# Gate and up products of two feed-forward layers as seven block products in place of eight

## The chip, the cores and the metric

The kernel runs on one core of one Trainium2 chip. The metric is the device time of one launch in microseconds, as the median of several runs. TensorE does the matmuls, VectorE (DVE in the profile), ScalarE (ACT) and GpSimd (POOL) the elementwise work, and SyncE (SP) issues most of the transfers.

## What is computed

One step of a decoder layer (model width 1024) for 1024 prompt positions and 64 sample positions, 1088 tokens together. The two feed-forward half steps stand at its beginning and at its end:

```python
def ffn_half_step(x, g, wg, wu, wd):
    h = rmsnorm(x, g)
    return x + 0.5 * ((jax.nn.silu(h @ wg) * (h @ wu)) @ wd)

# D_MODEL = 1024, D_FF = 2816
yp = ffn_half_step(yp, ffn1_norm[l], ffn1_gate[l], ffn1_up[l], ffn1_down[l])
...  # input projection, windowed attention, conformer convolution, output projection, cross attention
yp = ffn_half_step(yp, ffn2_norm[l], ffn2_gate[l], ffn2_up[l], ffn2_down[l])
```

The same two steps run on the sample tokens. All data are float32.

## The kernel before

Activations lie transposed: a channel is a partition, `T` = 1088 tokens are the columns. The channels make `KT` = 8 row tiles of 128. The tokens are cut into `CHUNKS` of 384, 384 and 320 columns. A float32 product is made of three fast matmuls: each operand is split into a high part (rounded to the format of the fast matmul) and the rest. The normed activations are `hh` and `hl`, the weights `wh` and `wl`, the hidden values `hidh` and `hidl`. The helper `three` (lines 778 to 781) issues high x high (L779), low weight x high (L780) and high weight x low (L781).

A feed-forward layer (`ffn`, one function on each engine) runs over `FG` = 11 groups of 256 hidden channels, the first ten of ffn2 and all of ffn1 as a hardware loop. In a group TensorE does, for two halves `f` of 128 hidden channels and for each chunk, the gate product and the up product (8 row tiles x 3 matmuls each) into two PSUM banks, and then the down products: for 3 chunks x 8 output tiles, 2 x 3 matmuls into one of the four banks 4 to 7. Beside it ScalarE applies silu to the gate (L1420), VectorE multiplies it with up into `ht` (L1933), ScalarE casts `ht` to `hidh` (L1426), VectorE subtracts to get `hidl` (L1921), and adds half of each down product to `x` (L1945), which frees the bank.

Weights: SyncE loads units of 128 x 1024 elements (512 KB) into the two buffers `raw` (`ffn_loads`, L470). GpSimd makes the high part with a cast (L718) and the rest with a subtraction (L720); `wh` and `wl` have four slots for gate and up, `bh` and `bl` two for down. All order comes from semaphores; each engine runs its own program. Before ffn1 TensorE transposes the convolution cache (`turn_cache`, L979) between the memory projections and the transposes of their results (L962); VectorE copies it to `Us`. After ffn1 comes a barrier and a norm, whose squares ScalarE makes (L1399) and TensorE sums (L788).

## Time and profile before

| | |
|---|---|
| median of 3 runs | 2730.72 us (2728.26 to 2732.05) |
| span of the profiled execution | 2729.7 us |
| TensorE busy | 2606.0 us, 95% |
| VectorE busy | 1085.0 us, 40% |
| GpSimd busy | 696.3 us, 26% |
| ScalarE busy | 546.1 us, 20% |
| ffn1 and ffn2, first matmul to last | about 99 to 891 us and 1902 to 2711 us |

The profile is of one execution. A line of a list of groups gives line, engine, operation, the output and input tiles, how often, then busy time and mean duration of one, then the idle time before them and what ended it. A line of a timeline gives start and duration in us. Matmuls overlap each other, so the sum of their durations is more than the time that they take. Spans on GpSimd are rough.

### The profile page before, as it was taken

Reading aid. Unit: us, or ns where it says so; the run is one execution under the profiler, and the core shown is the slowest. Engines: PE = TensorE matmul, PEld = TensorE weight load, DVE = VectorE, ACT = ScalarE, POOL = GpSimd, SP = SyncE. Lnnn points to the kernel's source line nnn. Section 1 sums busy time; section 2 is a strip of 40 time slices with the busy share of each in tenths; the row PEclk is TensorE's granted clock in tenths of the full one; section 3 lists DMA queues with packets and bytes.
Section 4 is the critical chain, followed back from the end, with each engine's and each line's share of the span. In section 5 each row is a group of like instructions: output and inputs, shape, how many; then the busy total and the mean of one; then the engine's idle time right before and its main releaser. Section 6 shows DMA issues by size and latency. Waiting matters only on the chain.

```text
span 2729.7 us, 42372 instructions
## 1 busy us (share of the span) xinstructions
PE 2606.0 (95%) x16775; PEld 2450.1 (90%) x16775; DVE 1085.0 (40%) x2019; ACT 546.1 (20%) x1307; POOL 696.3 (26%) x404
## 2 busy tenths in 40 slices
PE   7899999999999899979999999899899999999998
PEld 6899999999999799957557999679899999999998
DVE  5233323233332699544434343544422223233324
ACT  4200000000000415256323122321200000000002
POOL 6633222333223133123001220112333222333320
PEclk9999999999999999979999999999999999999999
DMA  6411111111111012145674223731111111111101
GB/s 214 130 46 42 38 43 46 46 46 38 38 46 46 16 46 94 43 170 171 258 287 134 62 72 122 291 127 46 47 46 42 38 42 46 46 46 46 38 23 66
DMA packets 208235, 224.48 MB, mean 82 GB/s; under 512 B 9978, under 2 KB 181558, under 8 KB 204051
## 3 DMA queue, kind: packets, MB, share of 16 engines
q1 hardware_dynamic: 191655, 195.45, 21.9%
q10 hardware_dynamic: 16492, 27.82, 2.7%
q8 instruction: 60, 0.98, 0.1%
q14 instruction: 28, 0.23, 0.0%
HBM read 190.84 MB, written 32.40 MB: 82 GB/s over the span
## 4 chain that ended last, share of the span: by engine, by line
PE 87%; DVE 6%; issue 3%; ACT 2%; DMA 2%; DVEq 0%; POOL 0%; SPq 0%; ACTq 0%; POOLq 0%
PE ps L779 25%; PE ps L781 24%; PE ps L780 24%; PE ps L1171 1%; PE ps L1215 1%; PE ps L1185 1%; PE ps L1099 1%; DVE hidl L1921 1%; PE ps L1112 1%; PE ps L1281 1%; PE ps L1264 1%; DVE ps L2017 1%; PE ps L1082 1%; DMA cK<-in_cache_mem_k 1%; DVE x L1945 0%
## 5 line engine op out<-in xcount | busy, mean ns | idle before, releaser
L779 PE MATMUL ps<-hh,wh 128*128 128x384 f32 (+1 forms) x3168 | 1041.5, 329 | 20.4 <-DVE ht L1933 6.3
L781 PE MATMUL ps<-hl,wh 128*128 128x384 f32 (+1 forms) x3168 | 1036.8, 327 | 0.0
L780 PE MATMUL ps<-hh,wl 128*128 128x384 f32 (+1 forms) x3168 | 1036.5, 327 | 0.0
L779 PEld LDWEIGHTS ps<-hh,wh 128*128 128x128 f32 x3168 | 597.7, 189 | 31.1 <-DVE hl L1887 8.6
L780 PEld LDWEIGHTS ps<-hh,wl 128*128 128x128 f32 x3168 | 598.1, 189 | 0.5
L781 PEld LDWEIGHTS ps<-hl,wh 128*128 128x128 f32 x3168 | 597.9, 189 | 0.0
L718 POOL CAST wh<-raw 128x1024 fp32r<-128x1024 f32 x148 | 154.3, 1042 | 1363.0 <-PE ps L781 1240.8
L1933 DVE TENSOR_TENSOR ht<-ps,sg 128x384 f32<-128x384 f32 x132 | 70.6, 535 | 925.9 <-PE ps L781 924.5
L720 POOL TENSOR_TENSOR wl<-raw,wh 128x1024 fp32r<-128x1024 f32 x148 | 367.4, 2482 | 11.9
L779 PE MATMUL ps<-hidh,bh 128*128 128x384 f32 (+1 forms) x1056 | 346.7, 328 | 11.7 <-DVE x L1945 11.7
L1945 DVE SCALAR_TENSOR_TENSOR x<-ps,x 128x384 f32<-128x384 f32 (+1 forms) x528 | 276.2, 532 | 185.6 <-PE ps L781 185.0
L781 PE MATMUL ps<-hidl,bh 128*128 128x384 f32 (+1 forms) x1056 | 344.5, 326 | 0.0
L780 PE MATMUL ps<-hidh,bl 128*128 128x384 f32 (+1 forms) x1056 | 344.3, 326 | 0.0
L1420 ACT ACTIVATE sg<-ps 128x384 f32<-128x384 f32 x132 | 62.5, 475 | 806.3 <-PE ps L781 806.1
L779 PEld LDWEIGHTS ps<-hidh,bh 128*128 128x128 f32 x1056 | 198.2, 188 | 18.4 <-DVE x L1945 18.4
L780 PEld LDWEIGHTS ps<-hidh,bl 128*128 128x128 f32 x1056 | 198.3, 188 | 0.0
L781 PEld LDWEIGHTS ps<-hidl,bh 128*128 128x128 f32 x1056 | 198.2, 188 | 0.0
L718 POOL CAST bh<-raw 128x1024 fp32r<-128x1024 f32 x44 | 46.0, 1046 | 447.7 <-PE ps L781 416.9
L2143 DVE SCALAR_TENSOR_TENSOR ps<-U,taps,ps 128x1024 f32<-128x1024 f32 x116 | 141.9, 1282 | 0.9
L1921 DVE TENSOR_TENSOR hidl<-ht,hidh 128x384 fp32r<-128x384 f32 x132 | 134.2, 1029 | 0.2
L1420 ACT ACT_TABLE_LOAD x20 | 25.7, 1283 | 503.2 <-PE ps L781 503.2
L720 POOL TENSOR_TENSOR bl<-raw,bh 128x1024 fp32r<-128x1024 f32 x44 | 105.7, 2402 | 3.5
(246 smaller groups left out, 2047.8 us busy)
## 6 DMA issues: line engine op xcount, KB each, us to landing
raw<-in_ffn_gate SPq DMA_DIRECT2D x44, 512.0 KB, 3.8
raw<-in_ffn_up SPq DMA_DIRECT2D x44, 512.0 KB, 3.8
raw<-in_ffn_down SPq DMA_DIRECT2D x44, 512.0 KB, 3.5
Kw<-in_cache_win_k SPq DMA_DIRECT2D x24, 512.0 KB, 6.0
Vw<-in_cache_win_v SPq DMA_DIRECT2D x24, 512.0 KB
raw<-in_w_in SPq DMA_DIRECT2D x20, 512.0 KB, 3.8
Kw<-in_cache_win_k SPq DMA_DIRECT2D x8, 1024.0 KB, 9.0
Vw<-in_cache_win_v SPq DMA_DIRECT2D x8, 1024.0 KB
```

Source lines behind the costliest of these rows:

```text
L718: pool.tensor_copy(hi, raw[:, parity]).then_inc(w_hi, 1)
L720: pool.tensor_tensor(lo, raw[:, parity], hi.bitcast(F32), ALU.subtract).then_inc(w_split, 1)
L779: pe.matmul(out, w_hi_, a_hi, start=first, stop=False)
L780: pe.matmul(out, w_lo_, a_hi, start=False, stop=False)
L781: return pe.matmul(out, w_hi_, a_lo, start=False, stop=last)
L1082: mm = pe.matmul(ps[:, 2 * h + n % 2, far(t):far(t) + near(t)], qs[64 * h:64 * h + 64, p, t * P:(t + 1) * P], kTp[64 * h:64 * h + 64, p, ( ...
L1099: mm = pe.transpose(ps[0:w, b, k * P:(k + 1) * P], Sb[:, n % 2, h, c:c + w], ident[:])
L1420: act.activation(sg[:, j % 2, 0:n], ps[:, 2 * (j % 2), 0:n], ACT.Silu).then_inc(s["sg"], 1)
L1921: dve.tensor_tensor(hidl[:, f, c0:c0 + n], ht[:, j % 2, 0:n], hidh[:, f, c0:c0 + n].bitcast(F32), ALU.subtract).then_inc(s["hid"], 1)
L1933: dve.tensor_tensor(ht[:, j % 2, 0:n], ps[:, 2 * (j % 2) + 1, 0:n], sg[:, j % 2, 0:n], ALU.mult).then_inc(s["prod"], 1)
L1945: dve.scalar_tensor_tensor(out=x[:, d, c0:c0 + n], in0=ps[:, 4 + j % 4, 0:n], scalar=0.5, in1=x[:, d, c0:c0 + n], op0=ALU.mult, op1=ALU.ad ...
L2143: dve.scalar_tensor_tensor(out=dst, in0=src, scalar=w, in1=acc, op0=ALU.mult, op1=ALU.add).then_inc(C["tap"], 1)
```

## The change

The tokens are halved at column 544 (`TH`), and each half is done in two pieces of 272 (`CW`), so that a pair of PSUM banks holds a half. The 8 row tiles are halved into 4 and 4, and the two 128-column halves `f` of a group's gate (or up) weights are the third halving. Each of gate and up is then a product of 2x2 blocks, and one level of Strassen's scheme (in Winograd's form) makes it with seven block products and additions around them:

- Sums and differences of the activation blocks are made once per layer: `th`/`tl` (three blocks of four row tiles), and a fourth that overwrites the second half of the lower four tiles of `hh`/`hl`. VectorE makes them (`differences`, `last_difference`), ScalarE casts (`turned`). While that goes on, the first group of each layer is done with the old eight products (`plain`), in the order chunk, then half `f`, gate before up.
- The other ten groups (`halved`) use seven products, of 4 row tiles x 3 matmuls x 2 pieces each. Three of the seven add onto a PSUM bank that holds an earlier one, which ScalarE has copied out before (`keep`). VectorE adds the copy to other products (`summed`).
- GpSimd makes four differences of weight quarters per matrix and cuts quarters of units: 128 x 512 elements, into a ring of six slots that gate, up and down share. SyncE loads quarters (256 KB). Separate slots for down are gone.
- The down products keep their number and widths; `hidl` is now made from a PSUM bank, not from `ht`. They run over the lower four output tiles of all chunks, then the upper four, save in the last group of ffn2.
- `turn_cache` and the copies to `Us` move from before ffn1 to after it; buffers of the attention stages are laid out anew; the load of the final gain moves behind ffn2's weights.

```diff
@@ TensorE
+            def halved(i, beside=None):
+                pp, cp, ad = s.base["pp"] + 28, s.base["up"], s.base["part"]
+                for w in range(2):
+                    one, two, three_ = ((0, 2, 4), (6, 4, 2))[w]
+                    for m in range(7):
+                        n = 7 * w + m
+                        pe.wait_ge(s["lo"], i * NS + (lo + NP + n + 1))
...
+                            if m == 0:
+                                mm = product(ps[:, one + c, 0:CW], n % RING, 0, 4, lambda k: hh[:, k, x0:x1],
+                                             lambda k: hl[:, k, x0:x1], True, True)
+                            elif m == 1:
+                                mm = product(ps[:, three_ + c, 0:CW], n % RING, 0, 4, lambda k: th[:, 0, k, x0:x1],
+                                             lambda k: tl[:, 0, k, x0:x1], True, True)
+                            elif m == 2:
+                                mm = product(ps[:, one + c, 0:CW], n % RING, 0, 4, lambda k: th[:, 1, k, x0:x1],
+                                             lambda k: tl[:, 1, k, x0:x1], False, True, True)
...
@@ VectorE
+            for k in range(3):
+                differences(k)
+            for j in range(2):
+                product(j)
+            for j in range(2):
+                lo(j)
+            differences(3)
+            for j in range(2, 6, 2):
+                product(j)
+                product(j + 1)
+                lo(j)
+                lo(j + 1)
+
+            def beside_first(c, d, j):
+                if j % 3 == 2:
+                    last_difference(j // 3)
+                    if j > 2:
+                        last_low(j // 3 - 1)
+
+            residual(0, lambda j: 4 + j % 4, False, beside_first)
...
+                def hidden(n, bank, f, t):
...
+                    for c in range(2):
+                        dve.wait_ge(s["hhi"], i * 8 + (hhi + 6 + 2 * n + c + 1))
+                        dve.tensor_tensor(part(hidl, f, t, c), ps[:, bank + c, 0:CW], part(hidh, f, t, c).bitcast(F32),
+                                          ALU.subtract).then_inc(s["hid"], 1)
+
+                summed(0, 0, lambda c: part(gated, 0, 0, c), 2, lambda c: part(gated, 0, 0, c))
...
+                summed(1, 0, lambda c: ps[:, 4 + c, 0:CW], 4, lambda c: part(parts, 0, 0, c))
+                hidden(0, 4, 0, 0)
+                summed(1, 1, lambda c: ps[:, 4 + c, 0:CW], 6, lambda c: part(parts, 1, 1, c))
+                hidden(1, 4, 1, 1)
+                summed(1, 2, lambda c: ps[:, 2 + c, 0:CW], 2, lambda c: part(parts, 1, 0, c))
+                hidden(2, 2, 1, 0)
+                hidden(3, 6, 0, 1)
@@ ScalarE
+            for j in range(4):
+                silu(j)
+            for q in range(6):
+                turned(q)
+            silu(4)
...
@@ GpSimd
+            def cut(q, r, n):
+                pool.tensor_copy(ring_hi(r), quadrant(q)).then_inc(s["whi"], 1)
+                pool.wait_ge(s["whi"], n)
+                pool.tensor_tensor(ring_lo(r), quadrant(q), ring_hi(r).bitcast(F32), ALU.subtract).then_inc(s["lo"], 1)
+
+            for n in range(NP):
+                q = n % 4 if n < 8 else (0, 2, 1, 3)[n - 8]
+                pool.wait_ge(s[f"in{q}"], s.base[f"in{q}"] + 16 * (n // 4 + 1))
+                if n < RING:
+                    pool.wait_ge(unit_done, UNIT[name] + n // 2 + 1)
+                else:
+                    pool.wait_ge(s["gate"], s.base["gate"] + {6: 5, 7: 5, 8: 6, 9: 6, 10: 11, 11: 11}[n])
+                cut(q, n % RING, lo + n + 1)
```

Where instructions move. TensorE, gate products inside a group, before (`hh`, `hl` are the activations, `wh`, `wl` the weights):

```order
L779 MATMUL ps<-hh,wh 128x384
L780 MATMUL ps<-hh,wl 128x384
L781 MATMUL ps<-hl,wh 128x384
L798 REGISTER_ALU
L779 MATMUL ps<-hh,wh 128x384
L780 MATMUL ps<-hh,wl 128x384
L781 MATMUL ps<-hl,wh 128x384
```

TensorE, in a halved group at the step from the first product to the second, after (L901 to L903 are the helper's new lines):

```order
L901 MATMUL ps<-hh,wh 128x272
L902 MATMUL ps<-hh,wl 128x272
L903 MATMUL ps<-hl,wh 128x272
L967 REGISTER_ALU
L971 ISA
L901 MATMUL ps<-th,wh 128x272
L902 MATMUL ps<-th,wl 128x272
L903 MATMUL ps<-tl,wh 128x272
```

Each product is issued in pieces of 272 columns over four row tiles, in place of 384 or 320 over eight.

VectorE, inside the first group of a layer, before:

```order
L1933 TENSOR_TENSOR ht<-ps,sg 128x384
L1921 TENSOR_TENSOR hidl<-ht,hidh 128x384
L1928 REGISTER_ALU
L1931 REGISTER_ALU
L1933 TENSOR_TENSOR ht<-ps,sg 128x384
```

VectorE, the third set of differences and the first two hidden tiles of the first group, after (`cell` and `parts` are scratch tiles in SBUF):

```order
L2161 TENSOR_TENSOR cell<-hh 128x272 x2
L2161 TENSOR_TENSOR cell<-cell,hl 128x272 x2
L2187 TENSOR_TENSOR cell<-cell,hl 128x272 x2
L2161 TENSOR_TENSOR parts<-cell,hh 128x272 x2
L2193 TENSOR_TENSOR parts<-parts,hl 128x272 x2
L2170 TENSOR_TENSOR tl<-cell,th 128x272 x2
L2161 TENSOR_TENSOR cell<-hh,parts 128x272 x2
L2202 TENSOR_TENSOR cell<-cell,hl 128x272 x2
L2170 TENSOR_TENSOR tl<-parts,th 128x272 x2
L2170 TENSOR_TENSOR tl<-cell,th 128x272 x2
L2227 TENSOR_TENSOR ps<-ps,gated 128x384 x2
L2233 TENSOR_TENSOR hidl<-ps,hidh 128x384 x2
```

Three such sets of 20 operations stand ahead of the first hidden tiles and a fourth behind them; the other 32 stand between the residual additions.

## Rows read from the trace of the kernel before

**Rows 1.** The page: busy time, the chain by engine and by line.

```profile
PE 2606.0 (95%) x16775; PEld 2450.1 (90%) x16775; DVE 1085.0 (40%) x2019; ACT 546.1 (20%) x1307; POOL 696.3 (26%) x404
...
PE 87%; DVE 6%; issue 3%; ACT 2%; DMA 2%; DVEq 0%; POOL 0%; SPq 0%; ACTq 0%; POOLq 0%
```

**Rows 2.** Stretch in ffn1: us; busy PE, PEld, DVE, ACT, POOL; clock; DMA share, GB/s.

```profile
700.00:800.00 100.00, 98.89 (x599) 98.25 (x597) 29.35 (x47) 9.56 (x20) 30.16 (x17) 1.00 0.17 49
```

**Rows 3.** Timeline of ScalarE: start us, duration us, operation [idle before <-releaser].

```profile
175.35 1.28 ACT L1420 ACT_TABLE_LOAD   x1 [27.64 <-PE ps L781]
...
247.28 1.28 ACT L1420 ACT_TABLE_LOAD   x1 [27.64 <-PE ps L781]
```

**Rows 4.** Timeline of TensorE at three widths, then the group of weight loads.

```profile
700.24 0.33 PE L779 MATMUL ps<-hh,wh 128*128 128x384 f32 x1
...
711.16 0.33 PE L779 MATMUL ps<-hh,wh 128*128 128x384 f32 x1
...
716.11 0.31 PE L779 MATMUL ps<-hh,wh 128*128 128x320 f32 x1
...
721.39 0.31 PE L779 MATMUL ps<-hh,wh 128*128 128x320 f32 x1
...
59.83 0.28 PE L779 MATMUL ps<-mh,wh 128*128 128x256 f32 x1
...
62.59 0.28 PE L781 MATMUL ps<-ml,wh 128*128 128x256 f32 x1
...
L779 PEld LDWEIGHTS ps<-hh,wh 128*128 128x128 f32 x3168 | 597.7, 189 | 31.1 <-DVE hl L1887 8.6 <-DVE hl L1994 7.2 <-issue 7.0
```

**Rows 5.** Waits of TensorE: total us, times, longest.

```profile
PE ps L779 <- DVE x L1945: 11.7, 21, 0.6
```

**Rows 6.** Groups by shape on GpSimd, VectorE and ScalarE.

```profile
L720 POOL TENSOR_TENSOR wl<-raw,wh 128x1024 fp32r<-128x1024 f32 x148 | 367.4, 2482 | 11.9
...
L2087 DVE TENSOR_TENSOR ml<-ps,mh 128x256 fp32r<-128x256 f32 x8 | 2.7, 412 | 3.4 <-ACT mh L1653 3.4
...
L1945 DVE SCALAR_TENSOR_TENSOR x<-ps,x 128x320 f32<-128x320 f32 x176 | 86.3, 491 | 65.8 <-PE ps L781 65.7
...
L1426 ACT CAST hidh<-ht 128x320 fp32r<-128x320 f32 x44 | 20.1, 456 | 74.0 <-DVE ht L1933 74.0
```

**Rows 7.** Timeline of VectorE and GpSimd at the end of a group's up products.

```profile
722.19 0.49 DVE L1933 TENSOR_TENSOR ht<-ps,sg 128x320 f32<-128x320 f32 x1 [6.01 <-PE ps L781]
722.60 3.62 DVE L1921 TENSOR_TENSOR hidl<-ht,hidh 128x384 fp32r<-128x384 f32 x2
...
722.16 1.04 POOL L718 CAST wh<-raw 128x1024 fp32r<-128x1024 f32 x1
723.28 2.58 POOL L720 TENSOR_TENSOR wl<-raw,wh 128x1024 fp32r<-128x1024 f32 x1
```

**Rows 8.** Timeline of VectorE and GpSimd beside the input projection.

```profile
943.51 1.62 DVE L2128 TENSOR_TENSOR U<-U,ya 128x1024 f32<-128x1024 f32 x1 [13.28 <-ACT ya L1471]
945.05 2.42 DVE L2130 TENSOR_TENSOR Us<-Us,ya 128x64 f32<-128x64 f32 x1
...
944.13 3.26 POOL L720 TENSOR_TENSOR wl<-raw,wh 128x1024 fp32r<-128x1024 f32 x1
...
955.99 2.40 POOL L720 TENSOR_TENSOR wl<-raw,wh 128x1024 fp32r<-128x1024 f32 x1
```

**Rows 9.** Busy time and granted clock at the start of ffn2.

```profile
1905.00:1950.00 45.00, 36.22 (x183) 33.54 (x182) 27.42 (x44) 12.96 (x27) 14.12 (x8) 0.88 0.17 47
```

**Rows 10.** Timeline before ffn1 and behind it.

```profile
82.22 0.55 DVE L2070 SCALAR_TENSOR_TENSOR ps<-x,vecs,ps 128x320 f32<-128x320 f32 x1
...
83.91 1.83 PE L979 MATMUL ps<-ident,cc_in 120*128 120x120 f32 x8 [3.96 <-DVE hl L2059]
...
85.53 2.95 PE L962 MATMUL ps<-ident,kvT 128*128 128x128 f32 x16
...
891.00 5.34 ACT L1399 ACTIVATE sq<-x 128x384 f32<-128x384 f32 x10 [23.96 <-DVEq L460]
```

More of the change, by code:

```diff
@@ L52 @@
 SLOTS = 4
+RING = 6
+TH = T // 2
+CW = TH // 2
+GAP = 128
 SQ = 4
@@ L309, in decoder_layer @@
     of_split = {"hi": NC * KT, "h": NC * KT} | {n: 16 for names in MIX for n in names}
-    of_ffn = {"gate": 4 * FG, "up": 4 * FG, "prod": 6 * FG, "res": NC * KT * FG, "sg": 6 * FG, "hhi": 6 * FG,
-              "hid": 6 * FG, "down": (NC * KT - 1) * FG}
+    NP, NS, ND = 12, 18, 4
+    REST = FG - 1
+    of_ffn = {f"in{q}": 16 * (2 + 1 + 3 * REST) for q in range(4)} | {
+        "whi": NP + NS * REST, "lo": NP + NS * REST, "mix": 8 * REST, "gate": 12, "pp": 28 * REST, "up": 12 * REST,
+        "part": 12 * REST, "sg": 6 + 8 * REST, "prod": 6 + 8 * REST, "hhi": 6 + 8 * REST, "hid": 6 + 8 * REST,
+        "down": NC * KT * FG, "res": NC * KT * FG, "sq": 48, "summed": 32, "var": 32, "rstd": 32}
     of_tiles = {"t": NC * KT, "hi": NC * KT, "h": NC * KT}
@@ L537, in _ @@
         sp.dma_start(taps_in[:], I["conv_w"].rearrange("o t c -> (o t) c")).then_inc(L["small"], 16)
-        load_kv(4)
+        for u in range(4, 16):
+            load_kv(u)
+        N1 = S["f1"]
+        ffn_loads("ffn1", N1)
+        sp.wait_ge(N1["pp"], N1.base["pp"] + 28 + 28 * REST)
         sp.dma_start(cc_in[:], cache_conv).then_inc(S["conv"]["cc_in"], 16)
-        for u in range(5, 16):
-            load_kv(u)
-        ffn_loads("ffn1")
+        sp.wait_ge(N1["lo"], N1.base["lo"] + NP + NS * REST)
         in_loads()
@@ L776, in _, with three @@
         pe.wait_ge(setup_done, 4)
-        def three(out, w_hi_, w_lo_, a_hi, a_lo, first, last):
-            pe.matmul(out, w_hi_, a_hi, start=first, stop=False)
-            pe.matmul(out, w_lo_, a_hi, start=False, stop=False)
-            return pe.matmul(out, w_hi_, a_lo, start=False, stop=last)
+        def three(out, w_hi_, w_lo_, a_hi, a_lo, first, last, more=False):
+            pe.matmul(out, w_hi_, a_hi, start=first, stop=False, skip_group_check=more)
+            pe.matmul(out, w_lo_, a_hi, start=False, stop=False, skip_group_check=more)
+            return pe.matmul(out, w_hi_, a_lo, start=False, stop=last, skip_group_check=more)
         def norm(s, chunks, sqt):
@@ L1007, in _ @@
         barrier(pe, 1)
-        ffn("ffn1", S["n1"])
+        ffn(S["f1"], S["n1"])
         barrier(pe, 2)
+        turn_cache()
         norm(S["nm"], CHUNKS, sq3)
+        pe.wait_ge(C["us"], CT)
         def ln_mean():
@@ L1366, in _ @@
         arrive(pe)
[L1368 removed]
+        F, N2 = S["fin"], S["f2"]
         def turn_out(t):
@@ L1948, in groups @@
                     if beside is not None:
-                        beside(c, d)
+                        beside(c, d, j)
+            for k in range(3):
+                differences(k)
+            for j in range(2):
+                product(j)
+            for j in range(2):
+                lo(j)
[10 more added lines that the diff above has]
+                        last_low(j // 3 - 1)
@@ L1951, in ffn @@
             if beside_last is None:
-                with dve.Fori(0, FG) as i:
-                    groups(i)
-            else:
-                with dve.Fori(0, FG - 1) as i:
-                    groups(i)
-                groups(FG - 1, beside_last)
+                with dve.Fori(0, REST) as i:
+                    halved(i)
+            else:
+                with dve.Fori(0, REST - 1) as i:
+                    halved(i)
+                halved(REST - 1, beside_last)
         def split_input(s):
```

604 lines of the change are left out of this document (422 added, 182 removed).

## The prediction

> **What bounds the kernel now.** I read the page's busy shares and its chain first, then the stretches of the two feed-forward layers. The page has TensorE busy for 95% of the span and on 87% of the chain that ended last, and three quarters of the chain are the three lines of one helper [rows 1]. In a stretch inside the first layer TensorE is busy 98.9 of 100 us, VectorE 29 and GpSimd 30 [rows 2]. So in the layers only two things can move the time: what TensorE has to issue, and what makes it wait. A group repeats every 71.93 us, from one ScalarE table load to the next [rows 3].
>
> Busy time says nothing on a matmul's price here, since matmuls overlap (one lasts 330 ns, the next starts 173 ns later). The pace does. From start to start, 63 matmuls of 384 columns take 10.92 us, 173.3 ns each; 36 of 320 columns take 5.28 us, 146.7 ns; 23 of 256 columns take 2.76 us, 120.0 ns [rows 4]. The three lie on one line: 120.0 + 0.4167 x (columns - 256) ns. A 272-column matmul should be paced at 126.7 ns.
>
> **Part 1: products of the ten halved groups, per layer.** Before, gate and up of a group are 4 units x 8 row tiles x 3 matmuls over widths 384, 384, 320: 96 x (173.3 + 173.3 + 146.7) ns = 47.36 us. Down is half of that, 23.68 us, together 71.04 us. The period has 0.89 us more. Of this 0.56 us is one wait per group for the residual addition, 21 waits and 11.7 us in all [rows 5]. Its cause is in the collision below; 0.33 us stay unexplained and I keep them. Now gate and up are 2 x 7 products x 2 pieces x 4 row tiles x 3 = 336 matmuls of 272 columns: 336 x 126.67 ns = 42.56 us. Down is unchanged. New period: 42.56 + 23.68 + 0.33 = 66.57 us, 5.36 us less. **20 x 5.36 = -107.2 us.**
>
> What has to keep up there:
> - GpSimd. A full unit costs 1.04 us of cast [rows 7] and on average 2.48 us of subtraction [rows 6], 2.40 undisturbed [rows 8]. Half units are not in the trace: at least half, 1.72 us, at most a whole, 3.44 us. I take half: the subtraction takes 2.3 times the cast, so the work sets the price and not a part that is the same for all. 18 half cuts and 8 half additions are 18 x 1.72 + 8 x 1.2 = 40.6 us of 66.6. A weight slot is refilled while TensorE does products of 3.04 us each, and only two of six slots wait for the end of the down products, whose users come 12 us into the group. Even at 2.5 us a cut (about 57 us) it would hold.
> - VectorE and ScalarE. A 272-column VectorE operation lies between 0.41 us (256 columns) and 0.49 us (320); ScalarE's cast of 320 columns took 0.46 us [rows 6]. I take 0.43 and 0.41. VectorE has 28 of these and 24 residual additions, 0.49 us at 320 columns [rows 6] and some 0.55 at 384, 25 us in all. Each product that reuses a bank waits for work on the product two or three back, one product (3.04 us) after it; copy plus semaphores need 0.6 us. The tightest place is the start of down: its first chunk needs the third hidden quarter, made from product 6 of 7 by addition, multiplication, cast and subtraction of two pieces, 8 operations in overlap, some 2.8 us, behind which TensorE has only product 7, 3.04 us. I price it at zero; if that cover is short it costs up to 1 us a group (third rival).
> - The wait of 0.56 us goes, because the subtraction that was late now reads PSUM. Late next is nothing: the fourth hidden quarter has 4.2 us of down products before it.
>
> **Part 2: the first group of each layer.** It keeps eight products, but in it VectorE and ScalarE also make the activation differences: 80 VectorE operations of 272 columns before the first residual, 32 between residuals, nearly all with both inputs in SBUF, and 32 casts. Here the trace speaks against the change. At 722.60 two VectorE subtractions with both inputs in SBUF took 3.62 us in place of about 1.0, and ended 0.36 us after GpSimd's subtraction; the multiplication at 722.19, one input from PSUM, took its normal 0.49 us beside a GpSimd cast [rows 7]. At 943.51 it goes the other way: GpSimd's subtraction lasted 3.26 us against 2.40 behind a VectorE product of two SBUF operands, and the next tiny VectorE one then lasted 2.42 us behind GpSimd [rows 8]. So the two exclude each other and alternate.
>
> I lay out the group from its first matmul, with back-to-back VectorE operations starting every 0.36 us (0.43 less an overlap: the operation of 0.49 us at 722.19 is followed after 0.41 [rows 7]). Products alone would end gate at 23.7, the fourth up piece at 40.3, up at 47.4, down at 71.0. ScalarE casts no difference before its fourth silu, at 17.2. From there VectorE has 50 operations to the first product of gate and up: 18 us, 35.2, so without a collision it is in time. But GpSimd makes 4 half cuts (8 operations, 7 us) from 20.2, and each lets one VectorE operation wait: 42.1, and the products, casts and subtractions release TensorE at 43.9, a stall of 3.6 us. Then come 20 operations, 7.2 us, against ten more GpSimd operations (9.3 us): 60.5, and the remaining hidden pieces until 64.7. TensorE has done up by 50.9 and four down pieces by 55.1, fills its four banks and waits for the first residual at 65.2: 10.2 us. The other 20 down pieces (19.6 us) then run 3.7 us slower, since VectorE has 24 residuals (11.4 us) and 32 operations (12.3 us) plus collisions. Sum 17.5 us; against the old group, whose wait of 0.56 goes, 16.9. **2 x 16.9 = +33.9 us.** Bounds: 0 (no collision: each of the waits is covered) to 34 us a layer: all of GpSimd's 25.4 us here (12 half cuts, 4 half additions) delay VectorE, 9.1 more than the 16.3 counted, and none of the 112 difference operations overlaps the next, 112 x 0.07 = 7.8. I take the laid-out schedule, as the collisions in the trace alternate just so.
>
> The clock: around the start of the second layer, where TensorE waits, its mean granted clock is 0.88 [rows 9], so some of the time at 1.2 GHz; inside ffn1 it is 1.00 [rows 2]. A stall of 10 us can bring one such dip per layer. Nothing if it falls into time that VectorE bounds, at most 3 us; I take 1 each: **+2 us.**
>
> **Part 3: around the layers.** The convolution cache's eight transposes leave the path into the first layer: they started at 83.91, after the last subtraction, and the key transposes behind them at 85.53. Those need only the last scaled tile, which ended at 82.77 [rows 10], and can start at 82.9. That is 2.6 us, and the output DMA and the last memory units behind it move along. They reappear after the layer, ahead of the norm's sums: 1.83 us, of which ScalarE's squares, from 891.00 on, cover the first 0.5 [rows 10]. **-2.6 + 1.3 = -1.3 us.** The four copies of VectorE fall into its wait for the sums. SyncE has 46 more, half-size loads a layer of the same bytes; they start when GpSimd frees a quarter of the buffer and have several products of cover. The relocated buffers and the later load of the final gain cost nothing: attention's waits stay, and the gain is needed 24 us after its load.
>
> **Sum:** -107.2 + 33.9 + 2.0 - 1.3 = -72.6 us against the profiled execution's span of 2729.7 gives 2657.1. The runs' median is 1.0 us above that span, which gives **2658.1 us**.
>
> **Rivals.**
> 1. *The differences are covered after all.* If VectorE in a stream gets the port before GpSimd, GpSimd alone is late, which has time. Then part 2 is 2 x -0.56 and the dips go: 2729.7 - 107.2 - 1.1 - 1.3 + 1.0 = 2621.1. For it: rows 8 begin with VectorE in possession. Against: GpSimd got in between two waiting VectorE operations there. The Trainium skill (SBUF — State Buffer, Who interferes with whom) says that issue order decides who is blocked, and for a whole instruction; the trace agrees with the second half and leaves open who wins in a stream.
> 2. *VectorE bears it all:* 34.4 us a layer, less 0.56, in place of 16.9: 2658.1 + 2 x 16.9 = 2692. For it: in rows 7 and 8 VectorE waits for whole GpSimd operations, 2.4 us each, though halved ones are shorter. Against: VectorE's operations do overlap in the trace, and part of GpSimd's work falls into VectorE's waits for ScalarE's casts.
> 3. *A handover per halved group,* at the start of down: +1 us x 20, 2678. For it: only 0.2 us of cover are left over. Against: the same chain of the old group, from its last product, is absorbed by four down pieces but for the collision.
> 4. *Slower:* the narrow matmuls do not follow the line. One matmul lasts 0.33 us at 384 columns, 0.31 at 320 and 0.28 at 256 [rows 4], so about 0.287 at 272, 0.87 of the wide one. If the pace shrinks only as that duration does (a fixed part per matmul that overlaps no further), it is 151 ns, and each of the 20 groups costs 336 x 24.3 ns = 8.2 us more: +163, 2821. It decides from 72.6 / (20 x 336) = 10.8 ns above the line, 137.5 ns. For it: 17% more matmuls and weight loads, of 189 ns each [rows 4]. Against: a load before each matmul kept up with a pace of 120 ns at 256 columns, and 272 lies between two measured widths. The Trainium skill (TensorE: Matmul & The Clock Gate, Back-to-back issue gap) gives a sustained spacing of about 81 ns at 128 columns and 131 ns at 512, a rule by which narrow matmuls pay a large fixed part: as an estimate, 272 columns would cost 0.87 of 384, the kernel again about 2821 us. The trace disagrees with it: the fixed part of its three paces is 13 ns.
> That the narrow products are not issued at all can be left out: the order of instructions shows them.
>
> **How the numbers follow.** Forecast 50%, rival 1 22%, rival 2 12%, rival 3 12%, rival 4 4%. The range must reach rival 1 below and most of rival 2 above: 2620 to 2692. A difference of 0.2% (5.5 us) is about what a measurement can tell from none. All cases but the fourth are faster by far more: faster 0.95, same 0.01, slower 0.04.
>
> **What would show it.** Right: 272-column matmuls paced at 126.7 ns; periods of 66.6 us; a first group of about 89 us, with TensorE waiting some 10 us for the first residual and differences of 0.9 to 1.6 us beside GpSimd's operations; no wait at the start of down. Wrong: a pace above 130 ns, waits inside the fourteen products, or a first group of 71 or of over 100 us.

## The result, and the profile after

The change takes the kernel from 2731.34 us (median of 4 runs, 2728.26 to 2732.05) to **2637.32 us** (median of 4, 2637.02 to 2644.49), 94.0 us less; ratio 0.9668, interval 0.9654 to 0.9682. The forecast was 2658.1, 72.6 us less: the sign and the range hold, the size is 21 us short. The profiled execution is the 2644.49 one.

The page after, busy time and chain [rows 1 before]:

```profile
span 2642.5 us, 48469 instructions
...
PE 2505.9 (95%) x17735; PEld 2350.0 (89%) x17735; DVE 1221.6 (46%) x2563; ACT 663.0 (25%) x1673; POOL 1189.8 (45%) x1068
...
PE 88%; DVE 5%; DMA 2%; ACT 2%; POOL 1%; issue 1%; SPq 0%; ACTq 0%; DVEq 0%; POOLq 0%
```

TensorE has 100 us less to do, by 960 more matmuls; GpSimd has 493 us more, and its share of the chain is now 1%, where it had rounded to 0. That GpSimd now stands on the chain is the first hint.

**The halved groups.** Timeline of ScalarE, the first copy of a halved group (start, duration, [idle before <-releaser]; the answer to [rows 3]), then TensorE at the first matmul of the halved group before it and at its first down product:

```profile
255.21 0.39 ACT L1645 COPY gated<-ps 128x272 f32<-128x272 f32 x1 [24.15 <-PE ps L903]
321.06 0.39 ACT L1645 COPY gated<-ps 128x272 f32<-128x272 f32 x1 [24.15 <-PE ps L903]
```

```profile
187.66 0.29 PE L901 MATMUL ps<-hh,wh 128*128 128x272 f32 x1
...
229.79 0.33 PE L901 MATMUL ps<-hidh,wh 128*128 128x384 f32 x1
```

The period is 65.85 us (forecast 66.57, before 71.93). The 336 matmuls of 272 columns take 229.79 - 187.66 = 42.13 us, 125.4 ns each; the down products take the other 23.72. TensorE waits nowhere in it.

The first copy of a group comes 1.70 us behind its first matmul, so the copy at 255.21 also tells where the first halved group began: 255.21 - 65.85 - 1.70 = 187.66. I use this below for the runs: **length of a first group = first copy of the second halved group - 67.55 - first matmul of the layer.** The formula holds where the first halved group runs without a wait. In ffn1 the length is 187.66 - 99.16 = 88.5 us, in ffn2 2030.52 - 67.55 - 1860.69 = 102.3 us. Before they were 71.9 and 87.8 (in ffn2 tiles of the norm are still being made; first matmul 1902.06, later table loads carried back by periods of 71.96).

**The first groups.** What TensorE waits for (total us, times, longest):

```profile
PE ps L901 <- POOL wl L793: 20.5, 2, 11.1
...
PE ps L901 <- DVE x L2244: 4.9, 2, 2.4
```

The wait of 0.56 us per group for a residual [rows 5] is gone but for two of 2.4. In its place TensorE waits 11.1 us in ffn1 and 9.4 in ffn2 for *weights*, which the forecast did not have. GpSimd in the first group of ffn1, then VectorE at the same time:

```profile
119.72 15.38 POOL L791 CAST wh<-raw 128x512 fp32r<-128x512 f32 x1 [22.56 <-PE ps L903]
135.18 1.26 POOL L793 TENSOR_TENSOR wl<-raw,wh 128x512 fp32r<-128x512 f32 x1
136.39 0.61 POOL L791 CAST wh<-raw 128x512 fp32r<-128x512 f32 x1
```

```profile
119.76 0.79 DVE L2170 TENSOR_TENSOR tl<-cell,th 128x272 fp32r<-128x272 f32 x2
120.47 0.78 DVE L2161 TENSOR_TENSOR cell<-hh 128x272 f32<-128x272 f32 x2
...
133.85 0.78 DVE L2170 TENSOR_TENSOR tl<-cell,th 128x272 fp32r<-128x272 f32 x2
134.55 0.56 DVE L2227 TENSOR_TENSOR ps<-ps,gated 128x384 f32<-128x384 f32 x1
```

A cast that takes 0.61 us lasts 15.38, until the last of VectorE's differences has ended and an operation with one input in PSUM follows. VectorE shows nothing: two operations in 0.79 us, one every 0.35. A reader who looks for a VectorE that is slow (as I did) finds none; the loss is on the other engine. In ffn2 it is the same:

```profile
1896.75 13.71 POOL L791 CAST wh<-raw 128x512 fp32r<-128x512 f32 x1 [48.15 <-PE ps L903]
```

TensorE behind the two places in ffn1:

```profile
138.39 0.69 PE L901 MATMUL ps<-hh,wh 128*128 128x384 f32 x1 [11.10 <-POOL wl L793]
...
178.29 0.44 PE L901 MATMUL ps<-hidh,wh 128*128 128x384 f32 x1 [2.44 <-DVE x L2244]
```

The granted clock in that group (us; busy PE, PEld, DVE, ACT, POOL; clock; DMA share, GB/s), the answer to [rows 9]:

```profile
130.00:141.00 11.00, 2.61 (x8) 2.61 (x9) 5.11 (x15) 2.17 (x6) 10.68 (x8) 0.56 0.14 48
141.00:150.00 9.00, 9.00 (x51) 9.00 (x51) 5.57 (x15) 2.02 (x5) 1.17 (x1) 0.97 0.22 60
150.00:171.00 21.00, 21.00 (x134) 20.96 (x133) 15.90 (x35) 3.42 (x8) 10.29 (x10) 1.00 0.09 26
171.00:183.00 12.00, 9.56 (x46) 9.11 (x46) 11.70 (x22) 1.26 (x3) 5.56 (x5) 0.86 0.00 0
```

Over the stretches that hold the two waits the mean clock is below 1.00, so it is at 1.2 GHz for part of them. In windows laid around it, the clock is 0.50 for 3.2 us behind the first wait (138.39 to 141.59) and for 3.4 us behind the second (179.13 to 182.55), while TensorE has work.

**The price of the small operations**, groups by shape, the answer to [rows 6]: 0.69 us mean for the half cast (0.61 undisturbed), 1.29 us for the half subtraction (forecast 0.52 and 1.20), 0.44 for VectorE's 272 columns (0.43):

```profile
L793 POOL TENSOR_TENSOR wl<-raw,wh 128x512 fp32r<-128x512 f32 x384 | 496.5, 1293 | 30.8
L791 POOL CAST wh<-raw 128x512 fp32r<-128x512 f32 x384 | 264.6, 689 | 528.7 <-PE ps L903 462.0 <-POOL raw L823 27.0 <-DMA raw<-in_ffn_down 20.4
...
L2294 DVE TENSOR_TENSOR hidl<-ps,hidh 128x272 fp32r<-128x272 f32 x160 | 64.8, 437 | 8.6
```

**The entry.** TensorE ahead of ffn1, the answer to [rows 10]:

```profile
84.33 3.73 PE L1149 MATMUL ps<-ident,kvT 128*128 128x128 f32 x16 [2.98 <-DVE ps L2427]
...
99.16 0.44 PE L901 MATMUL ps<-hh,wh 128*128 128x384 f32 x1 [1.27 <-ACTq L492]
```

The key transposes start 1.2 us earlier than at 85.53, but take 3.73 us in place of 2.95, at 421 ns each, the duration of the lower clock level (272 ns at the upper one, some 10 us later), and the next four row tiles of the memory unit are at that level too. ffn1 starts at 99.16, 0.3 later than before. TensorE also came to this wait later, at 81.35 us for 79.95 before.

**The account** of the profiled execution: halved groups 20 x -6.08 = -121.6; first groups +16.6 and +14.5; entry +0.3; the stretch between the layers (from ScalarE's first square behind ffn1 to the first matmul of ffn2) +2.7, from 1011.1 to 1013.8 us, and the last group of ffn2 with what follows it some +1: -86.5, and the spans say 2729.7 - 2642.5 = 87.2.

### The profile page after: what moved, and what is told of

Its sections match the earlier page's. It is cut to its first block, busy times and chain, and to the rows that moved or that the text cites. A ratio compares the mean times of both kernels' runs of the same rounds, so it can differ in the third digit from the quotient of the medians.

```text
span 2642.5 us, 48469 instructions
## 1 busy us (share of the span) xinstructions
PE 2505.9 (95%) x17735; PEld 2350.0 (89%) x17735; DVE 1221.6 (46%) x2563; ACT 663.0 (25%) x1673; POOL 1189.8 (45%) x1068
## 4 chain that ended last, share of the span: by engine, by line
PE 88%; DVE 5%; DMA 2%; ACT 2%; POOL 1%; issue 1%; SPq 0%; ACTq 0%; DVEq 0%; POOLq 0%
PE ps L901 25%; PE ps L902 25%; PE ps L903 25%; PE ps L1358 1%; PE ps L1402 1%; POOL wh L791 1%; PE ps L1372 1%; PE ps L1286 1%; PE ps L1299 1%; DMA cK<-in_cache_mem_k 1%; PE ps L1468 1%; PE ps L1451 1%; DVE ps L2376 1%; PE ps L1269 1%; DVE hl L2353 0%
## 5 line engine op out<-in xcount | busy, mean ns | idle before, releaser
L901 PE MATMUL ps<-hh,wh 128*128 128x272 f32 (+2 forms) x2528 | 784.6, 310 | 41.8 <-POOL wl L793 20.5
L902 PE MATMUL ps<-hh,wl 128*128 128x272 f32 (+2 forms) x2528 | 780.9, 309 | 0.0
L903 PE MATMUL ps<-hl,wh 128*128 128x272 f32 (+2 forms) x2528 | 780.8, 309 | 0.0
L901 PEld LDWEIGHTS ps<-hh,wh 128*128 128x128 f32 x2528 | 479.9, 190 | 53.5 <-POOL wl L793 21.2
L793 POOL TENSOR_TENSOR wl<-raw,wh 128x512 fp32r<-128x512 f32 x384 | 496.5, 1293 | 30.8
L903 PEld LDWEIGHTS ps<-hl,wh 128*128 128x128 f32 x2528 | 478.7, 189 | 0.0
L901 PE MATMUL ps<-hidh,wh 128*128 128x384 f32 (+1 forms) x1056 | 345.6, 327 | 4.9 <-DVE x L2244 4.9
L903 PE MATMUL ps<-hidl,wh 128*128 128x384 f32 (+1 forms) x1056 | 345.2, 327 | 0.0
L902 PE MATMUL ps<-hidh,wl 128*128 128x384 f32 (+1 forms) x1056 | 344.9, 327 | 0.0
L902 PE MATMUL ps<-th,wl 128*128 128x272 f32 x960 | 277.2, 289 | 0.0
L901 PE MATMUL ps<-th,wh 128*128 128x272 f32 x960 | 276.1, 288 | 0.0
L903 PE MATMUL ps<-tl,wh 128*128 128x272 f32 x960 | 275.9, 287 | 0.0
L901 PEld LDWEIGHTS ps<-hidh,wh 128*128 128x128 f32 x1056 | 198.8, 188 | 6.0 <-DVE x L2244 5.8
L903 PEld LDWEIGHTS ps<-hidl,wh 128*128 128x128 f32 x1056 | 198.7, 188 | 0.0
```

The costliest lines, as they stand in the source:

```text
L793: pool.tensor_tensor(ring_lo(r), quadrant(q), ring_hi(r).bitcast(F32), ALU.subtract).then_inc(s["lo"], 1)
L901: pe.matmul(out, w_hi_, a_hi, start=first, stop=False, skip_group_check=more)
L902: pe.matmul(out, w_lo_, a_hi, start=False, stop=False, skip_group_check=more)
L903: return pe.matmul(out, w_hi_, a_lo, start=False, stop=last, skip_group_check=more)
```

## Experiments

Lengths of the first groups (us) and the medians, each beside runs of the kernel before on the same chip (2730.6 to 2732.1). The lengths go from the layer's first matmul to the first one of 272 columns. In e6 and e9 TensorE also waits inside the first halved group; there the formula above gives some 6 us more (in brackets), which belong to that group.

| kernel | ffn1 | ffn2 | median us | ratio, interval |
|---|---|---|---|---|
| the change | 88.5 | 102.3 | 2637.3 | 0.9668 (0.9654 to 0.9682) |
| e1_cast_order | 77.1 | 102.1 | 2628.5 | 0.9625 (0.9609 to 0.9641) |
| e2_yield | 82.5 | 95.5 | 2627.7 | 0.9619 (0.9603 to 0.9635) |
| e3_narrow | 71.2 | 86.4 | 2600.6 | 0.9519 (0.9503 to 0.9535) |
| e6_all_orders | 79.3 (85.9) | 92.2 (98.4) | 2627.5 | 0.9625 (0.9609 to 0.9641) |
| e7_cover | 88.4 | 101.9 | 2659.4 | 0.9735 (0.9719 to 0.9751) |
| e8_psum_cells | 74.2 | 90.6 | 2611.6 | 0.9569 (0.9553 to 0.9585) |
| e9_psum_orders | 72.5 (77.9) | 87.6 (94.2) | 2618.6 | 0.9587 (0.9571 to 0.9603) |
| e10_psum_all | 72.1 | 86.0 | **2602.3** | 0.9535 (0.9521 to 0.9550) |
| e11_chained | 98.2 | 112.4 | 2658.1 | 0.9742 (0.9717 to 0.9766) |

The theory is that an unbroken stream of VectorE operations with two SBUF inputs keeps GpSimd out until it ends. The rival is VectorE's load and its alternation with GpSimd, as forecast. A weight cut is GpSimd's cast and subtraction for one weight quarter.

**e1_cast_order.** ScalarE in ffn1's first group:

```diff
-            for j in range(4):
-                silu(j)
-            for q in range(6):
-                turned(q)
+            for q in range(6):
+                turned(q)
+            silu(0)
+            for q in range(6, 12):
+                turned(q)
...
```

> The changed kernel, but in ffn1's first group ScalarE casts the first differences ahead of its first silus, so that VectorE's unbroken stream of differences lies at about 103 to 124 us in place of 117 to 134; ffn2 as it is. Theory (a stream of VectorE operations with two SBUF inputs keeps GpSimd out until it ends, and its place decides): the cut that GpSimd begins at 119.7 ends at about 124.5 in place of 135, TensorE's wait of 11.1 us for the weights falls to 0 to 2, ffn1's first group lasts 73 to 76 us in place of 88.5, the time is 12 to 16 us less, about 2623. Rival (the load on VectorE and its alternation with GpSimd set the group's length wherever the stream lies, as I forecast): the wait goes over to the first residual, the group stays above 84 us, the time at or above 2633.

VectorE's stream ran from 99.3 to 120.5; GpSimd:

```profile
115.55 5.41 POOL L791 CAST wh<-raw 128x512 fp32r<-128x512 f32 x1 [20.19 <-PE ps L903]
121.05 1.28 POOL L793 TENSOR_TENSOR wl<-raw,wh 128x512 fp32r<-128x512 f32 x1
```

The cast ends 0.5 us behind the stream's last operation (120.96 for 120.49), as in the change (135.10 for 134.63), wherever the stream lies. The wait for weights is 1.15 us, the group 11.4 shorter. It is still 5.7 above 71.4: the 2.4 us for a residual stayed, with a lower clock behind it. The theory held, but the gain was smaller than expected: 8.8 us in the median for 12 to 16, and a first group of 77.1 for 73 to 76.

**e2_yield.** VectorE gives way once:

```diff
             for k in range(3):
+                if k == 2:
+                    dve.wait_ge(s["lo"], s.base["lo"] + 8)
                 differences(k)
```

> The changed kernel, but in both first groups VectorE waits, ahead of its third set of differences, until GpSimd has made the seventh and eighth weight cuts. Nothing is left out; VectorE loses about 3.8 us by it. Theory (stream keeps GpSimd out): the waits for weights of 11.1 and 9.4 us fall to about 0 in ffn1 and 3 to 5 in ffn2, in their place come 1 to 5 us for the first hidden tile or the first residual: 8 to 16 us less in all, 2621 to 2629. Rival (VectorE's load sets the length): what the weights give back the later hidden tiles take, within 3 us of 2637. If VectorE and GpSimd alternate in a stream, the edit changes nothing.

The waits for weights fell to 4.0 and 2.6 us, the time by 9.7: within the theory's 8 to 16, near its lower end. The cast lasted 8.34 us, until VectorE stopped.

**e3_narrow.** Part of the sums left out:

```diff
-                dve.tensor_tensor(out, a, b, op).then_inc(s["sq"], 1)
+                w = cols[0]
+                dve.tensor_tensor(out[:, 0:w], a[:, 0:w], b[:, 0:w], op).then_inc(s["sq"], 1)
...
+                cols[0] = 16 if k else CW
...
```

> The changed kernel with part of the computation left out: in the second to fourth set of differences and in the last ones, 66 of VectorE's additions and subtractions per layer work on 16 of 272 columns; the first set and all subtractions of the high parts stay whole. It takes about 66 x 0.28 = 18 us of VectorE's work from each first group. Theory (stream keeps GpSimd out): the stream in ffn1 ends at about 127 in place of 134, or has gaps that let GpSimd in before; the wait for weights falls from 11.1 to under 5, no wait for a residual; together 12 to 24 us less, 2613 to 2625. Rival (VectorE's load alone): the whole surplus of the first groups over 71.4 us goes, 17.1 and 14 with the dips, at least 28 us less, under 2609.

The time is below the theory's range: 36.7 us less, as the rival had it, with first groups of 71.2 and 86.4. It prices the whole at 17.3 + 15.9 us, but does not tell the causes apart: the short operations also let GpSimd in (the cast took 1.32 us). The run moved both suspects at once.

**e5_psum_product.** One part of the change in the kernel before:

```diff
-                    dve.tensor_tensor(ht[:, j % 2, 0:n], ps[:, 2 * (j % 2) + 1, 0:n], sg[:, j % 2, 0:n], ALU.mult
+                    dve.tensor_tensor(ps[:, 2 * (j % 2) + 1, 0:n], ps[:, 2 * (j % 2) + 1, 0:n], sg[:, j % 2, 0:n], ALU.mult
                                       ).then_inc(s["prod"], 1)
-                    if j >= 1:
-                        lo(j - 1)
+                    lo(j)
...
```

> The kernel before with one part of the change alone: the product of silu(gate) and up stays in its PSUM bank, ScalarE casts and VectorE subtracts from there, so the subtraction has one SBUF input in place of two. Theory: the wait of 0.56 us for a residual in each group (21 waits, 11.7 us) goes, 2731 becomes about 2720. Rival (the late subtraction is late for another reason, or the next VectorE operation with two SBUF inputs takes the collision over): no change, 2728 to 2732.

2714.8 us against 2732.1, ratio 0.9941 (0.9924 to 0.9957), more than the expected 11 us. Its table loads in ffn1, then VectorE and GpSimd at the end of a group's up products:

```profile
243.22 1.28 ACT L1420 ACT_TABLE_LOAD   x1 [26.84 <-PE ps L781]
314.32 1.28 ACT L1420 ACT_TABLE_LOAD   x1 [26.84 <-PE ps L781]
```

```profile
216.42 0.49 DVE L1919 TENSOR_TENSOR hidl<-ps,hidh 128x320 fp32r<-128x320 f32 x1 [0.49 <-ACT hidh L1426]
...
216.52 2.41 POOL L720 TENSOR_TENSOR wl<-raw,wh 128x1024 fp32r<-128x1024 f32 x1
```

The period is 71.10 us, and 71.04 are matmuls: not only the wait of 0.56 went, but also the 0.33 that I could not explain. So that went with the same wait. The edit also changes an order, which the expectation does not say: the subtraction of the fifth tile moves ahead of the sixth product, so that one and no longer two subtractions stand before the residuals. The one that is left takes 0.49 us beside GpSimd's subtraction, but how much of the gain is the PSUM input and how much the order is not shown. The change's halved groups have no such wait either, so some 17 of its 94 us could be had without seven products in place of eight.

**e6_all_orders.** e1's order in ScalarE, a wait as in e2 but inside a set, and two of eight last differences behind the residuals:

```diff
+                if k == (2 if s is S["f1"] else 1):
+                    dve.wait_ge(s["lo"], s.base["lo"] + 8)
...
-                if j % 3 == 2:
+                at = (2, 6, 9, 13, 16, 20)
+                if j in at:
...
+            for n in (6, 7):
+                last_difference(n)
+                last_low(n - 1)
```

> The changed kernel with three changes of order in the first groups and the same work: ScalarE's order of the first run; VectorE waits in the middle of a set of differences (the third of ffn1, the second of ffn2) until GpSimd has made the seventh and eighth weight cuts; two of the eight last differences move from between the residuals to behind them. Theory (GpSimd is kept out by the stream, VectorE's load matters only where it is packed against a need): ffn1's first group 72 to 74 us (77.1 with the first order alone, 88.5 in the changed kernel), ffn2's 86 to 89 in place of 102.3: 2605 to 2614. Rival (VectorE's load alone bounds the group): what the order gives back at one wait comes again at the first hidden tile or residual, ffn2's first group stays above 95 and the time above 2618.

Neither expectation came true as a whole: the time is no better than that of e1 or e2 and above the rival's bound of 2618, while ffn2's first group, 92.2, is below the rival's 95. The waits for weights were gone (0.2 us), but TensorE now waited 4.7 us in ffn1 for a silu, which stood in ScalarE's program behind casts of differences that VectorE had put off, and 3.6 us in each layer for the first copy of the next group, behind the casts of the last differences. In ffn2 it also waited 2.5 us for a hidden tile and 2.4 for residuals, where the rival had put the loss. The orders had made new waits, so this run does not decide between the two.

**e8_psum_cells.** The same sums, the scratch tiles in idle PSUM banks:

```diff
-                a = [cell[:, c, :] for c in range(2)]
-                b = [part(parts, c, 1, 1) for c in range(2)]
+                a = [ps[:, 4 + c, 0:CW] for c in range(2)]
+                b = [ps[:, 6 + c, 0:CW] for c in range(2)]
```

(with the signals to ScalarE one step later, so that the two engines never read one bank together, and two more waits for the banks: of VectorE ahead of the first set, of TensorE ahead of the down products)

> The changed kernel with the scratch tiles of the four sets of differences in PSUM banks 4 to 7, which are idle at that time, in place of SBUF; same sums, same number of operations. 2 of 20 operations of a set still have two SBUF inputs, the others one. Theory (what keeps GpSimd out is an unbroken stream of VectorE operations with two SBUF inputs): GpSimd's cast inside the stream takes 0.6 to 1.4 us in place of 13.7 to 15.4, both waits for weights go (11.1 and 9.4 us), something of 1 to 5 us for the first residual stays; 18 to 26 us less, 2611 to 2619. Rival (any stream of VectorE that touches SBUF keeps GpSimd out): no change, 2634 to 2641. Rival (VectorE's load bounds): under 8 us less.

GpSimd inside the stream, then VectorE there:

```profile
117.25 0.62 POOL L791 CAST wh<-raw 128x512 fp32r<-128x512 f32 x1 [21.48 <-PE ps L903]
117.95 1.57 POOL L793 TENSOR_TENSOR wl<-raw,wh 128x512 fp32r<-128x512 f32 x1
```

```profile
116.54 1.47 DVE L2171 TENSOR_TENSOR tl<-ps,th 128x272 fp32r<-128x272 f32 x4
117.93 1.89 DVE L2162 TENSOR_TENSOR ps<-hh 128x272 f32<-128x272 f32 x2
119.74 1.48 DVE L2162 TENSOR_TENSOR ps<-ps,hl 128x272 f32<-128x272 f32 x4
```

VectorE does as many operations at the same pace, and the cast takes 0.62 us. Only the pair with both inputs in SBUF (`ps<-hh`) is longer, 1.89 in place of 0.79. The time is 25.7 us less, within the theory's 18 to 26, and both waits for weights are gone; the load stayed, so the rival's "under 8 us" is out. The clock in ffn1's first group was granted at 1.00. What stayed is 2.43 us for a residual:

```profile
159.62 1.41 DVE L2218 TENSOR_TENSOR cell<-cell,hl 128x272 f32<-128x272 f32 x1
160.96 1.50 DVE L2171 TENSOR_TENSOR hl<-cell,hh 128x272 fp32r<-128x272 f32 x1
...
159.37 1.36 POOL L793 TENSOR_TENSOR wl<-raw,wh 128x512 fp32r<-128x512 f32 x1
160.69 1.46 POOL L823 TENSOR_TENSOR raw<-raw 128x512 f32<-128x512 f32 x1
```

Here the two do alternate, one for one, as I had forecast for the whole group.

**e10_psum_all.** e8, and the cells of the last differences in banks 2 and 3:

```diff
-                at = then(cell[:, c, :], h12, h11, ALU.subtract, 0)
-                at = then(cell[:, c, :], cell[:, c, :], l12, ALU.add, at)
+                at = then(ps[:, 2 + c, 0:CW], h12, h11, ALU.subtract, 0)
+                at = then(ps[:, 2 + c, 0:CW], ps[:, 2 + c, 0:CW], l12, ALU.add, at)
```

> The kernel with scratch tiles in PSUM (2611.6), and with those of the last differences, between the residual additions, in the idle banks 2 and 3 too; one of their four operations still has two SBUF inputs. There TensorE still waits 2.4 us for a residual in each layer, behind VectorE operations of 1.4 to 1.5 us that waited for GpSimd's. Theory (they alternate where VectorE's operations depend on each other, because both inputs are in SBUF): these last 0.45 us, the wait falls to under 0.5; the first groups last 71.5 to 72.5 and 87.5 to 89 us, the time 2605 to 2609. Rival (VectorE's plain load between residuals is the bound): the wait stays, 2610 to 2613.

VectorE, then GpSimd, beside the residuals:

```profile
159.79 0.45 DVE L2220 TENSOR_TENSOR ps<-ps,hl 128x272 f32<-128x272 f32 x1
160.15 0.43 DVE L2171 TENSOR_TENSOR hl<-ps,hh 128x272 fp32r<-128x272 f32 x1
...
159.81 1.29 POOL L793 TENSOR_TENSOR wl<-raw,wh 128x512 fp32r<-128x512 f32 x1
```

The operations with one SBUF input take their normal time beside GpSimd, and the wait is gone in both layers. The first groups are 72.1 and 86.0 us and the time 2602.3, a little under what was expected. It is the fastest version with nothing left out, 128 us under the kernel before and 35 under the change. Its first groups last about as long as those of e3 (71.2 and 86.4), which left 18 us of VectorE's work out of each. So nearly all that e3 saved was the collision and not the load.

**e9_psum_orders.** e8 with e1's order and e6's last differences:

> The scratch tiles in PSUM together with ScalarE's order in ffn1 and two last differences behind the residuals; VectorE waits nowhere for GpSimd. Theory: ffn1's first group 71.5 to 73 us, ffn2's 86 to 88, 2603 to 2611, a little under the version that makes VectorE wait. Rival (the placing alone matters): the same as that version or slower.

The first groups are as long as expected (72.5 and 87.6 us), but the time, 2618.6, is above the expected 2611 and 7 us above e8's. The residual wait fell to 0.9, and in the halved group behind it a wait for the copy came:

```profile
178.63 0.39 PE L901 MATMUL ps<-th,wh 128*128 128x272 f32 x1 [3.62 <-ACT gated L1659]
```

The casts of the last differences came at 173.69 and 177.88, and ScalarE's first copies for the halved group, which its program has behind them, at 178.20. This and e6 place the fault in the late differences.

**e11_chained.** Why alternate here and not there? In the sets, two independent pieces overlap (0.44 us each, a start every 0.35); the last differences depend on each other.

```diff
+            def chained(name, value):
+                if last:
+                    dve.wait_ge(*last[0])
+                last[:] = [(s[name], value)]
...
+                chained("sq", step[0] + 1)
...
```

> The changed kernel, each VectorE operation of the sets of differences made to wait for the one before it: same operations, order and SBUF tiles, but none overlaps the next (a start every 0.47 us in place of 0.35). Theory (VectorE keeps GpSimd out only while its operations overlap; in a gap GpSimd gets one operation in, then VectorE one): GpSimd's cast inside the stream takes 0.6 to 1.4 us in place of 13.7 to 15.4, VectorE's operations beside it 1.0 to 1.5; the waits for weights of 11.1 and 9.4 us go, in their place TensorE waits for hidden tiles or residuals since VectorE needs some 8 us more for the sets and 8 more beside GpSimd; the time 2630 to 2650. Rival (it is the number of waiting VectorE operations, or VectorE's rank at the port): the cast again lasts until the stream ends, later than before: 2645 to 2665.

```profile
117.69 0.61 POOL L791 CAST wh<-raw 128x512 fp32r<-128x512 f32 x1 [22.30 <-PE ps L903]
118.38 1.37 POOL L793 TENSOR_TENSOR wl<-raw,wh 128x512 fp32r<-128x512 f32 x1
119.70 0.82 POOL L791 CAST wh<-raw 128x512 fp32r<-128x512 f32 x1
```

```profile
118.70 2.11 DVE L2179 TENSOR_TENSOR tl<-parts,th 128x272 fp32r<-128x272 f32 x2
120.92 2.11 DVE L2179 TENSOR_TENSOR tl<-cell,th 128x272 fp32r<-128x272 f32 x2
...
127.34 0.99 DVE L2197 TENSOR_TENSOR cell<-cell,hl 128x272 f32<-128x272 f32 x2
```

GpSimd gets in at once and VectorE pays: 2.11 us for two beside GpSimd, 0.99 alone. The waits for weights are gone; those for a hidden tile (9.5) and for residuals (10.0) are in ffn1 what I had forecast as 3.6 and 10.2, the first much larger; a chained operation starts every 0.55 us in place of 0.35. The time, 2658.1, came out above the theory's 2650 and inside the rival's 2645 to 2665, but the rival's sign, a cast that lasts until the stream ends, did not come. So my forecast described this kernel in kind, not the one that was written. Whether it is the dependence or the short gap between operations that lets GpSimd in, this run does not tell.

**e7_cover.** Four more operations ahead of the start of the down products:

```diff
+                        if n == 2:
+                            dve.wait_ge(s["sg"], i * 8 + (sg + 6 + 8))
+                            for out in (cell[:, c, :], ps[:, c, 0:CW]):
+                                dve.tensor_tensor(out, ps[:, bank + c, 0:CW], part(gated, f, t, c), ALU.mult)
```

> The changed kernel with four more VectorE operations of 272 columns in each halved group, in the chain that makes the third hidden quarter, for which the down products start; results unused. By the trace the chain ends 0.55 us before it is needed, and four operations take 4 x 0.36 = 1.44 us. If that cover is all there is: TensorE waits 0.9 us in each of 20 groups, 18 us more, about 2655. If the cover is 0.2 us, as I forecast: 25 us more, 2662. If the operations lie beside the waits for ScalarE's casts and cost little: under 8 us more.

The end of the chain in the change, then in this run with the first down product behind it:

```profile
228.45 0.79 DVE L2294 TENSOR_TENSOR hidl<-ps,hidh 128x272 fp32r<-128x272 f32 x2
```

```profile
229.42 0.98 DVE L2298 TENSOR_TENSOR hidl<-ps,hidh 128x272 fp32r<-128x272 f32 x2
...
230.54 0.43 PE L901 MATMUL ps<-hidh,wh 128*128 128x384 f32 x1 [0.81 <-DVE hidl L2298]
```

This group began at 187.44 us, that of the change at 187.66. Counted from there the chain ended 1.38 us later (42.96 for 41.58) and the first down product started 0.97 us later (43.10 for 42.13). The cover, the time by which the chain had been early, was therefore 1.38 - 0.97 = 0.41 us, and TensorE's wait is 0.81. The period grew by 1.06 to 66.91 us, the time by 22 (2659.4), between the expected 18 and 25: the wait and a quarter of a microsecond more.

## Why the prediction was right and wrong

- **Pace of the narrow products:** right. The forecast was 126.7 ns, measured were 125.4. 336 x 20 times the difference is -8.5 us. Rival 4 (a large fixed part per matmul, 151 ns) is out.
- **Period:** "0.33 us stay unexplained and I keep them" is the step that failed: 20 x 0.33 = 6.6 us. e5 shows that they went with the wait. With the pace this makes 15 of the 21 us by which the forecast was short.
- **The 0.56 us wait goes** since the subtraction reads PSUM: the wait went, in e5 too. That the PSUM input is the reason is not shown alone, since e5 also moves a subtraction forward.
- **Start of down priced at zero** (rival 3): right. The cover was 0.4 us, not 0.2; in e7, 0.97 us beyond it cost 1.06 us per group.
- **GpSimd in the halved groups keeps up:** right, at 1.90 us a half cut in place of 1.72. TensorE does not wait there.
- **First groups:** 2 x 16.9 forecast, 16.6 and 14.5 measured, and the mechanism was wrong. The step that failed: "So the two exclude each other and alternate", "each lets one VectorE operation wait". They exclude each other, but VectorE's overlapping stream did not let GpSimd in. The forecast had 3.6 us for the product, 10.2 for the first residual and 3.7 in down; found were 11.1 and 9.4 us for weights, 2.4 for a residual, and lost clock. That the sums agree is chance. The sign I had named, differences of 0.9 to 1.6 us beside GpSimd, did not come in the stream, where two last 0.79. The places of [rows 7] and [rows 8] could not tell: no stream of overlapping two-SBUF operations stands there.
- **Rival 1** had right who wins at the port, the access to SBUF at which the two exclude each other ("VectorE in a stream gets the port before GpSimd") but had the consequence wrong ("GpSimd alone is late, which has time"): from GpSimd's request at 119.7 to TensorE's need for the eighth cut at 138.39 - 11.10 = 127.3 there were 7.6 us, and the first of the two casts alone took 15.4. The Trainium skill (SBUF — State Buffer, Who interferes with whom) says that the order of issue decides who is blocked. The profile has the cast begun at 119.72, ahead of some 40 of VectorE's operations, and all of these went first: in a stream the trace does not agree. In a chain of dependent operations (e11) it agrees. The Trainium skill says in the same section that a VectorE instruction with at most one SBUF input does not contend with GpSimd. The trace agrees: with an operand in PSUM the cast took 0.62 us (e8).
- **Rival 2** (VectorE bears it all, 33.8 us a layer): out for this kernel. e11, with 26.3 and 24.6 us, lies between it and the forecast.
- **Clock:** forecast +1 us a layer. ffn1's first group is 17.5 above its matmuls' 71.0, its waits are 13.5; e8 has 0.8 left over beyond its wait at a clock of 1.00, the change 3.9. So the clock took some 3 us in ffn1, which fits the 6.6 us in which TensorE worked at 1.2 GHz there (half of that is lost). In ffn2 the group is 16.3 above e10's with 11.8 of extra waits; 4.5 are left, of which the clock's part was not separated.
- **Entry and exit:** forecast -2.6 + 1.3. With the transposes TensorE waits 4.0 us ahead of them, and from there to ffn1 it takes 15.0 and 15.2 us (before, e5). Without them the wait is 3.0 us, and the way takes 13.9 us where the clock was low for as long as in those two (e1, e3, e8, e9), 14.7 to 14.8 where it was low for longer (the change, e2, e7, e10, e11) and 12.9 where it stayed up (e6). So at the same clock 2.1 to 2.3 of the 2.6 us came. The profiled execution of the change had the longer low stretch, and it reached the wait 1.4 us later, behind a longer low stretch at 25 us: +0.3 in place of -2.6. The 1.3 behind the layer can't be seen: the stretch between the layers varied from 1005.9 to 1013.8 us among profiles of kernels that don't differ there.
- **Sum** of the differences from the forecast: periods -14.4; first groups with their clock 31.1 - 35.8 = -4.7; entry +2.9; the rest +2: -14 in the profiled execution, whose span went down by 87.2 in place of 72.6. The median went down by 94.0, since that execution is 7 us above the other three. These have no profile, so where they saved 7 us stays open. In the twelve profiles the entry ended between 94.6 and 99.2 us, mostly the later the longer the clock stayed low at 25 us, and the stretch between the layers spread by 8: either is large enough. By its number rival 1 (2621.1) is nearer to the measured 2637.3 than the forecast (2658.1); neither names the wait for weights.

## What to carry to other kernels

A helper job of VectorE was cheap here only where it left GpSimd the port: look for a GpSimd operation that lasts many times its normal, not for a slow VectorE, and put one operand of every VectorE operation into an idle PSUM bank. Breaking the stream up by a wait gave 9.7 us (e2), the tiles in PSUM 25.7 (e8). Moving the stream's tail on top of that cost 7 (e9), since the engine that serves it (here ScalarE, in program order) carries the delay to others. When a period has a small remainder that the matmuls don't explain, consider that it goes with the wait beside it, and multiply it by the number of groups before calling it small.

## What the runs showed of the hardware that was not expected

- Overlapping VectorE operations with two SBUF inputs held GpSimd's 0.61 us cast for 15.38 and 13.71 us, without any loss of their own; with dependent operations the same cast took 0.61, and two of VectorE's took 2.11 beside GpSimd's in place of 0.99; with one input in PSUM in 18 of 20 operations the cast took 0.62, and only a pair with two SBUF inputs lost time (1.89 in place of 0.79).
- Matmuls of 272 columns were paced at 125.4 ns, 1.3 below the line through 256, 320 and 384.
- A wait of 3 us ahead of the key transposes was followed by 16 transposes at 421 ns and by matmuls of 256 columns at 410 ns in place of 272 and 280. That taking the cache's transposes out of this place lowers the clock is not shown: of the ten profiles without them, the 16 key transposes took 3.73 us in five, 3.27 in four and 2.45 in one, and in the two with them 2.95 and 3.25.
